# Three modulation pairs of the first block's second projection: from TensorE to VectorE

## The reference, cut to what matters

```python
c_act = jax.nn.silu(c)                                  # (1, 1024)
mod = c_act @ w_ada[l] + b_ada[l]                       # (1, 9 * 1024)
sh1, sc1, g1, sh2, sc2, g2, sh3, sc3, g3 = split(mod, 9)
u = _modulate(_rmsnorm(h, norm_ffn1[l]), sh1, sc1)
h = h + 0.5 * g1 * _swiglu(u, w_ffn1_up[l], w_ffn1_down[l])
u = _modulate(_rmsnorm(h, norm_mix[l]), sh2, sc2)
h = h + g2 * _hybrid_mixer(u, w_in[l], ...)
```

## Time and profile before

| | us |
|---|---|
| median of 3 runs | 1413.84 |
| lowest, highest | 1411.04, 1415.01 |
| the profiled execution | 1410.68 |
| its span in the trace | 1408.8 |

### The profile page before, as it was taken

The page is one execution under the profiler, slowest core; times in us unless marked ns, Lnnn a source line. Parts: engine busy times, 40 slices in busy tenths (PEclk is TensorE's granted clock), DMA queues, the critical chain, the costliest instruction groups (busy, mean ns, idle before and its releaser), DMA issues.

```text
span 1408.8 us, 28238 instructions
## 1 busy us (share of the span) xinstructions
PE 1350.3 (96%) x11721; PEld 1220.1 (87%) x11721; DVE 901.8 (64%) x1385; ACT 714.5 (51%) x1163; POOL 739.7 (53%) x821
## 2 busy tenths in 40 slices
PE   6999999999999998999999999899999999999998
PEld 2788887888888888978888999878999999888998
DVE  4888735787898458666544586576634675776433
ACT  2555533775446334454555547555544565555432
POOL 0777653343234224646557575356656443677653
PEclk9999999999999999999999999999999999999999
DMA  9887687553334433557555754346565444555560
GB/s 364 292 268 261 225 294 281 180 161 100 119 120 151 153 119 108 186 187 238 191 191 169 232 172 150 120 150 192 179 218 186 154 135 135 162 183 194 180 209 31
DMA packets 234612, 258.58 MB, mean 184 GB/s; under 512 B 8489, under 2 KB 211703, under 8 KB 234359
## 3 DMA queue, kind: packets, MB, share of 16 engines
q1 hardware_dynamic: 230272, 252.22, 53.9%
q10 hardware_dynamic: 4215, 4.58, 1.1%
HBM read 255.71 MB, written 2.63 MB: 183 GB/s over the span
## 4 chain that ended last, share of the span: by engine, by line
PE 79%; DVE 13%; ACT 3%; issue 2%; DMA 2%; POOL 0%; DVEq 0%; SPq 0%; ACTq 0%
PE ps L723 35%; PE ps L717 23%; PE ps L719 11%; DVE w_lo L1957 3%; PE ps L988 2%; DMA raw<-in_w_ffn_up 1%; PE ps L679 1%; DVE mt L2214 1%; DVE arow L1985 1%; ACT w_hi L1341 1%; DVE sil L2214 1%; DMA raw<-in_w_ada 1%; DVE sil L2063 1%; PE ps L1032 1%; DVE mt L2121 0%
## 5 line engine op out<-in xcount | busy, mean ns | idle before, releaser
L651 POOL TENSOR_TENSOR w_lo<-raw,w_hi 128x256 fp32r<-128x256 f32 x800 | 724.5, 936 | 651.7 <-ACT w_hi L1341 651.7
L1341 ACT CAST w_hi<-raw 128x1024 fp32r<-128x1024 f32 (+1 forms) x408 | 411.8, 1045 | 179.7 <-PE ps L723 110.8
L717 PE MATMUL ps<-u_hl,w_hi 128*128 128x512 f32 x1216 | 427.3, 396 | 13.3 <-DVE w_lo L1957 5.8
L1957 DVE TENSOR_TENSOR w_lo<-raw,w_hi 128x1024 fp32r<-128x1024 f32 x204 | 275.2, 1349 | 124.4 <-ACT w_hi L1341 123.0
L723 PE MATMUL ps<-u_hl,w_hi 128*128 128x256 f32 x1856 | 348.5, 289 | 5.0 <-POOL w_lo L651 1.8
L719 PE MATMUL ps<-u_hl,w_lo 128*128 128x256 f32 x1216 | 339.3, 279 | 0.0
L723 PEld LDWEIGHTS ps<-u_hl,w_hi 128*128 128x128 f32 x1856 | 289.7, 192 | 18.9 <-issue 8.3
L717 PEld LDWEIGHTS ps<-u_hl,w_hi 128*128 128x128 f32 x1216 | 227.8, 187 | 72.2 <-issue 17.5
L723 PE MATMUL ps<-u_hl,w_lo 128*128 128x256 f32 x928 | 263.4, 284 | 0.0
L719 PEld LDWEIGHTS ps<-u_hl,w_lo 128*128 128x128 f32 x1216 | 229.3, 189 | 0.1
L723 PE MATMUL ps<-mid_hl,w_hi 128*128 128x256 f32 x1024 | 180.8, 280 | 0.0
(11 more groups left out here) (375 smaller groups left out, 1531.0 us busy)
## 6 DMA issues: line engine op xcount, KB each, us to landing
raw<-in_mlp_w SPq DMA_DIRECT2D x64, 1024.0 KB, 5.0
raw<-in_w_ffn_up SPq DMA_DIRECT2D x44, 1024.0 KB, 4.9
raw<-in_w_ada SPq DMA_DIRECT2D x36, 1024.0 KB, 5.4
raw<-in_w_in SPq DMA_DIRECT2D x30, 1024.0 KB, 5.1
raw<-in_w_ffn_down SPq DMA_DIRECT2D x16, 1024.0 KB, 5.1
raw<-in_attn_w_in SPq DMA_DIRECT2D x12, 1024.0 KB, 5.1
raw<-in_mlstm_w_in SPq DMA_DIRECT2D x12, 1024.0 KB, 5.0
raw<-in_w_ffn_down SPq DMA_DIRECT2D x8, 768.0 KB, 4.3
```

Of the source, the lines that this page charges most:

```text
L651: pool.tensor_tensor(w_lo[half][:, kt, :], src[:, kt, :], w_hi[half][:, kt, :].bitcast(F32), ALU.subtract).then_inc(low_ready(n, h)[0], 1)
L717: pe.matmul(two(b - 10 + m), x, z, start=(first and kt == ks.start), stop=False, skip_group_check=True)
L1341: act.copy(w_hi[t % HALVES][:, 0:k, :], src).then_inc(hi_ready, 1)
L1957: dve.tensor_tensor(w_lo[half][:, 0:k, :], src, w_hi[half][:, 0:k, :].bitcast(F32), sub)\
```

## The change

Pairs 9, 10 and 11 go from `BY_TENSOR` to `BY_VECTOR`. Their eight operations each are put inside groups 0, 1 and 2 of the first block's down projection: three behind the first `ahead`, three behind the second, two behind the third. Their loads enter the list one group earlier, since VectorE takes pair 9 in group 0, while TensorE took it behind group 0. Pair 12 stays as it was. `mod_out` stays at its place.

```diff
+            if (name, g) in INSIDE:
+                plan.ada(INSIDE[name, g])
             for q in range(3):
                 plan.weight((name + "d", g, q), down, 8 * q, min(8, KF - 8 * q), g * SLAB)
...
-ADA = {"f1": ({0: 4, 2: 5, 4: 6, 6: 7, 8: 8}, {0: 9, 1: 10, 2: 11, 3: 12}, {1: 9, 2: 10, 3: 11, 4: 12}),
+ADA = {"f1": ({0: 4, 2: 5, 4: 6, 6: 7, 8: 8}, {3: 12}, {1: 9, 2: 10, 3: 11, 4: 12}),
        "f2": ({1: 17}, {}, {})}
-BY_VECTOR = (4, 5, 6, 7, 8, 17)
-BY_TENSOR = (2, 3, 0, 1, 9, 10, 11, 12, 13, 14, 15, 16)
+BY_VECTOR = (4, 5, 6, 7, 8, 9, 10, 11, 17)
+BY_TENSOR = (2, 3, 0, 1, 12, 13, 14, 15, 16)
+INSIDE = {("f1", 0): 9, ("f1", 1): 10, ("f1", 2): 11}
...
                 for g in range(4):
+                    p = INSIDE.get((name, g))
+                    row = itertools.chain(rows(p, 0), rows(p, 1)) if p is not None else iter(())
                     for q in range(3):
                         ahead(plan.slab[(name + "d", g, q)])
+                        for _ in range((3, 3, 2)[q]):
+                            next(row, None)
```

More of the change, by code:

```diff
@@ L9 @@
 import concourse.bass as bass
+import itertools
 import numpy as np
```

## The result

| | before | changed |
|---|---|---|
| median of 4 runs, us | 1412.44 | 1439.26 |
| lowest, highest | 1410.3, 1415.01 | 1437.58, 1443.99 |
| the profiled execution | 1410.68 | 1437.58 |
| its span | 1408.8 | 1435.8 |

The changed kernel is slower by 26.8 us, ratio 1.0193 with a 95% interval of 1.0173 to 1.0214. The forecast was 1442.8 in a range of 1430 to 1453.

A forecast was written before the change was run, and what follows sets the result against it. TensorE was taken to bound the stage, then to wait for late slab loads: stage 28.2 us longer, relief included, plus 0.8 for the clock, about +29. 1410.68 + 29 = 1439.7, plus 3.2 to the median: 1442.8 us, range 1430 to 1453.

The forecast's parts named there:

- The held buffer and the list: Down projection: VectorE returns pair buffers late and SyncE's in-order list holds slab loads behind them; two waits per group, chance 0.77.
- The walk: Step-by-step times from 173.6 us through the down projection's groups, ending at 264.65 against 236.45 us: stage 28.2 us longer.
- first release: VectorE's fourth product, behind the low half of slab 0.2, frees `raw1` at 179.25 us, so slab 1.0 can load.
- second release: VectorE's last operation of the group, behind slab 1.0's low half, frees `raw2` at 189.55 us.
- turn of 28.65 us: One loop of loads, low halves and VectorE products per group takes 28.65 us, where TensorE before needed 17.8.
- sign of being wrong: Prediction wrong if slab 1.1 is issued before slab 1.0's low half is written, or the stage ends before 245 us.
- the third of three loads: Slab 1.1, issued behind two halves of a pair, lands 10.4 us after the first issue, between 9.0 and 11.0.
- tensor_scalar: One added VectorE operation per pair, ahead of its seven scalar_tensor_tensor, taken at 0.49 us.
- the lone load: A slab load with nothing ahead of it, from issue to landing: 5.7 us, from readings of 5.0, 5.6 and 6.6.
- The clock: TensorE's clock drops after long waits; hidden inside the loop, only the last slabs count: 0.8 us added, giving +29.
- The rival of the low clock: Clock mostly 0.5 from 187 to 250 us puts TensorE on the path: +45 to +55, 1459 to 1469 us; chance 0.05.
- The relief: Three pairs' products leave TensorE in the down projection: net 4.5 us less work, which falls into its waits for loads.

The follow-up runs named there:

- keep the list and release at once: Changed kernel's load order, but pairs 9 to 11 multiplied on TensorE, which gives both buffers back behind slab g.0: 1411.83 us, 0.9997 of the kernel before.
- both cures: Changed kernel with pair halves loaded behind slabs g.1 and g.2 and VectorE's eight operations spread 4, 4, 0, not 3, 3, 2: 1407.48 us, 0.9963 of the kernel before.
- (4, 4, 0): Changed kernel with a pair's eight VectorE operations spread 4, 4, 0 over a group's three steps, not 3, 3, 2: 1419.45 us, 1.0049 of the kernel before.
- small pairs: Changed kernel with only 64 of 512 columns of pairs 10 and 11 loaded: 1430.06 us, 1.0121 of the kernel before.
- later loads: Changed kernel with a pair's halves listed behind slabs g.1 and g.2, not both behind g.0; operations untouched: 1411.33 us, 0.9996 of the kernel before.
- idle work: Kernel before plus 24 VectorE operations at the changed kernel's places, on a spare tile nobody reads: 1412.54 us, 0.9997 of the kernel before.

## Why the prediction was right

- **The held buffer and the list** carried the forecast, and three experiments show it from three sides: give back sooner (+11.5 us of stage in place of +29.35), ask later (-0.8), keep the list and release at once (0.0).
- **The walk.** Its times against those of the chain: first release 179.25 forecast, 179.7 measured; slab 1.0's low half ready 187.25, 187.18; second release 189.55, 189.46; slab 1.1's low half 202.25, 203.1; end of group 3 264.65, 265.9. The turn of 28.65 us was 209.2 - 179.7 = 29.5 and then 237.4 - 209.2 = 28.2. SyncE issued slab 1.1 at 191.27, behind the low half of slab 1.0, and the stage ended well after 245 us: neither sign of being wrong came.
- **A term that was too small:** the third of three loads. It landed 11.4 us after the release in the first turn, above the upper end of 11.0. SyncE needed 1.8 us for the two issues ahead, one of which took 1.2 us. In the second turn it was 229.05 - 218.84 = 10.2, near the 10.4 forecast. The prediction's working does not give its own figure: 2.5 us for each further megabyte and 0.2 for the spacing are 5.7 + 5.2 = 10.9, and not 5.7 + 2 x 2.35.
- **A second term that was too small:** the tensor_scalar took 0.96 us in each group, not 0.49; four of the five of that row had run while GpSimd was idle. It stands on the path, ahead of each release of the first half, and made the way from the low half to this release 6.1 us in place of 5.65, three times: 1.3 us in all. The products took 1.11 to 1.16, as assumed at 1.15.
- **A term that was too large:** the lone load. At slabs 1.0, 2.0, 3.0 and 3.1 it took 4.92 to 5.05 us, not 5.7. Of the three loads of the earlier trace rows only the first was alone: half a pair had gone out at 177.31 us, ahead of the second, and at 206.40, ahead of the third. Over the four this is 2.9 us.
- **Luck.** These errors, +0.8 us for the third loads over two turns, +1.3 and -2.9, and the slow last slabs of the next point, +1.7, nearly cancelled. The mechanism did not depend on it; that the stage came within 1.2 us of the walk did.
- **The clock.** It fell more than the 0.8 us of the prediction suggest, to a mean of 0.79 from 187 to 250 us. Slab 1.0 took from 187.28 to about 195.6, 8.3 us in place of 5.6, so that the second wait was 7.6 us and not 9.4, and all waits of TensorE from 183 to 262 us were 23.3 and not 35; at slab 3.0 there was none. The rival of the low clock asked for a clock of mostly 0.5 from 187 to 250 us, and that did not come. Inside the loop the slow stretches used up TensorE's own waits, as forecast. The last slabs paid: 3.1 and 3.2 took from 254.39 to about 265.9, 11.5 us in place of 9.8, at a mean clock of 0.57 from 254 to 258 us. That is 1.7 us, where 0.8 was taken.
- **The relief** of 4.5 us was real but hidden, as forecast: the kernel with both cures shows it, 3.8 us in the stage and 5.1 in the median.
- **What was not foreseen:** the stage lost 29.35 us and the program 26.9 in the profiled executions (1437.58 - 1410.68). From the residual of group 3 to the end of the span it took 1408.8 - 236.45 = 1172.35 us before and 1435.8 - 265.92 = 1169.9 after. In the eight other kernels, whose code there is the same but for pairs 10 and 11, this rest was between 1168.3 and 1175.0 us, one execution each. The kernel before had a stretch of 0.90 and 0.93 of the clock from 360 to 380 us that the changed one did not have in the same place; whether that is the whole difference is not shown. So the 2.5 us lie within what one execution of the rest varies, and I do not read them as a gain of the change. The forecast was 3.5 us too high. 2.1 of these are in the profiled execution (1439.7 against 1437.58), where the stage was 0.35 longer than the forecast +29 and the rest 2.5 shorter. The other 1.5 are the step from it to the median, taken as 3.2 us and measured as 1.7.

The Trainium skill was weighed at two places. The rule that the prediction cites from the page "SBUF — State Buffer" of the Trainium skill (section "Summary: rules for kernel authors") gives no size; the trace agrees with it in kind. Beside GpSimd a product took 1.11 to 1.16 us in the changed kernel. With (4, 4, 0) the last three of a group run while GpSimd is idle and take 0.76:

```profile
179.54 1.23 DVE arow L1989
180.79 0.76 DVE arow L1989
181.58 0.76 DVE arow L1989
182.37 0.76 DVE arow L1989
```

By the fit in the page "DMA: Bandwidth & Descriptors" (section "Anatomy of one DMA — SWDGE (gpsimd) path") of the Trainium skill a lone load would be 4.4 us, an estimate for another issue path. The eight lone ones in the chains of the changed kernel and of the one with small pairs took 4.82 to 5.05 us, nearer to this than to the 5.7 of the prediction. For the third of three the estimate is 9.2 us, and the changed kernel took 11.4 and 10.2.

## What to carry to other kernels

When work moves from one engine to another, ask who gives the input buffer back, after what, and which load stands behind it in the queue that issues in order. In this kernel a buffer that was returned late cost next to nothing by itself, as the later loads show; it cost when a load that the bounding engine needs waited behind it, and most when its return in turn depended on such a load. The cure was cheap: put the load whose buffer is held longest behind the ones that are urgent, and place the last use ahead of any wait for the next load. Both cures together turned a loss of 27 us into a gain of 5.

## What the runs showed of the hardware

- TensorE had no steady clock in this loop of short work and long waits. After its 3.6 us wait the granted clock of the changed kernel was 0.50 from 187.3 to 192.5 us, the lower level of 1.2 GHz, though TensorE was busy without a gap; the prediction had read three microseconds of this from the earlier trace rows. It then rose to full, was down at 0.50 in the last 3 us of the 7.6 us wait, and stayed there from 203.2 to 206.5 us:

```profile
187.20:193.20 6.00, 5.92 (x19) 5.13 (x20) 4.57 (x7) 0.00 (x0) 3.54 (x4) 0.53 0.45 130
193.20:203.10 9.90, 2.43 (x14) 1.85 (x13) 1.14 (x1) 2.19 (x3) 0.15 (x1) 0.83 0.89 320
203.00:208.00 5.00, 4.76 (x19) 4.12 (x20) 4.89 (x6) 1.47 (x2) 5.00 (x5) 0.65 0.00 0
```

- One late load stands in three engines' wait lists at once. From 183 to 262 us of the changed kernel GpSimd waited 48.1 us for ScalarE, VectorE 38.3 for ScalarE, and ScalarE 64.3 for the loads.
- A tensor_scalar of 128x512 from a load buffer took 0.96 us behind a low half in all three groups, with GpSimd at its own low halves. At four of its five places in the up projection it starts while GpSimd is idle, and took 0.49 in every kernel. At the first place GpSimd is at work too, but no low half of VectorE stands directly ahead: there it took 0.98 in the changed kernel and up to 1.06 in four others, and 0.49 to 0.53 in the kernel before and the rest. So a low half ahead is not needed for the longer time, and without GpSimd it never came; why it sometimes stays away beside GpSimd is open.
- Doubling VectorE's busy time raised GpSimd's from 33.2 to 42.2 us for the same 40 or so operations (the idle work against the kernel before, 171 to 236 us), and TensorE was busy in 64.75 of the 65 us in both.
